# Gate operands of a two-layer decoder trunk: one of five formed in the gates, VectorE's gate steps in another order

## The reference

```python
    for i in range(DEPTH):                      # DEPTH = 2
        ...                                     # mixer of the layer, layer_norm
        hid = jnp.square(jax.nn.relu(jnp.einsum('bsd,df->bsf', x, ffn_w1[i])))
        x = layer_norm(DEEPNORM_ALPHA * x + jnp.einsum('bsf,fd->bsd', hid, ffn_w2[i]), ln2_g[i], ln2_b[i])
        gate = jax.nn.sigmoid(jnp.einsum('bsd,de->bse', x, ple_gate_w[i]))
        x = x + gate * jnp.einsum('bsk,kd->bsd', p[i], ple_w[i])
```

## Time and profile before

| | us |
|---|---|
| median of 3 runs | 2057.95 |
| lowest, highest | 2057.12, 2059.17 |
| profiled execution, own time | 2063.47 |
| profiled execution, span | 2061.7 |
| TensorE (PE) busy | 2036.8 |
| VectorE (DVE) busy | 1405.0 |
| ScalarE (ACT) busy | 890.9 |
| GpSimd (POOL) busy | 763.4 |

### The profile page before, as it was taken

How to read it: one execution, slowest core, us unless ns; L and a number is a source line. 1 busy time by engine, 2 the same in 40 slices (tenths; PEclk the granted TensorE clock), 3 DMA queues, 4 the chain that set the end, 5 groups by cost and what they waited for, 6 DMA issues and landing times.

```text
span 2061.7 us, 25116 instructions
## 1 busy us (share of the span) xinstructions
PE 2036.8 (99%) x9341; PEld 1689.1 (82%) x9341; DVE 1405.0 (68%) x1721; ACT 890.9 (43%) x1283; POOL 763.4 (37%) x505
## 2 busy tenths in 40 slices
PE   9999999999999999999999999999999999999999
PEld 9888788888888888787888888788888888887877
DVE  4744775655666868676887669775655666777595
ACT  3112465455544445352433343654444543445541
POOL 5212257777702000110367650268877412000200
PEclk9999999999999999999999999999999999999999
DMA  6121123444589896434122238033443599886343
GB/s 190 38 66 41 41 75 129 159 159 147 203 288 390 301 321 224 167 112 153 42 77 87 88 114 308 21 117 139 160 155 135 207 380 383 281 296 226 113 174 123
DMA packets 201366, 352.19 MB, mean 171 GB/s; under 512 B 14401, under 2 KB 72861, under 8 KB 198685
## 3 DMA queue, kind: packets, MB, share of 16 engines
q1 hardware_dynamic: 190432, 320.92, 44.5%
q10 hardware_dynamic: 10812, 29.67, 3.9%
HBM read 258.78 MB, written 91.75 MB: 170 GB/s over the span
## 4 chain that ended last, share of the span: by engine, by line
PE 79%; DVE 11%; issue 3%; POOL 3%; ACT 2%; DMA 1%; DVEq 0%; ACTq 0%; POOLq 0%
PE bank_a L2735 15%; PE bank_a L2737 15%; PE bank_a L2736 15%; PE bank_b L2735 10%; PE bank_b L2737 10%; PE bank_b L2736 10%; POOL op_lo L1457 2%; DVE hop_lo L2521 1%; DMA w_raw<-in_ffn_w_dram 1%; DVE wop_lo L2524 1%; PE bank_a L2774 1%; PE bank_b L2774 1%; POOL op_sum L1548 1%; DVE xt_lo L2021 1%; DVE xt_lo L2221 1%
## 5 line engine op out<-in xcount | busy, mean ns | idle before, releaser
L1444 POOL TENSOR_TENSOR w_lo<-raw,w_hi 128x512 fp32r<-128x512 f32 x84 | 118.3, 1440 | 694.6 <-ACT w_hi L1569 694.5
L1457 POOL TENSOR_TENSOR op_lo<-op_sum,op_hi 128x512 fp32r<-128x512 f32 x151 | 224.5, 1503 | 33.4 <-ACT op_hi L1891 27.5
L1891 ACT CAST op_hi<-op_sum 128x512 fp32r<-128x512 f32 x151 | 93.8, 621 | 328.9 <-POOL op_sum L1548 87.9
L1856 ACT CAST hop_hi<-h_raw 128x1024 fp32r<-128x1024 f32 x124 | 130.3, 1051 | 231.2 <-PE bank_a L2737 134.7
L2735 PE MATMUL bank_a<-wop_hi,hop_hi 128*128 128x512 f32 x576 | 224.4, 390 | 0.4 <-DVE resid L2543 0.4
L2736 PE MATMUL bank_a<-wop_lo,hop_hi 128*128 128x512 f32 x576 | 224.3, 389 | 0.0
L2737 PE MATMUL bank_a<-wop_hi,hop_lo 128*128 128x512 f32 x576 | 224.3, 389 | 0.0
L2521 DVE TENSOR_TENSOR hop_lo<-h_raw,hop_hi 128x1024 fp32r<-128x1024 f32 x124 | 152.0, 1226 | 97.4 <-ACT hop_hi L1856 97.2
L1457 POOL TENSOR_TENSOR op_lo<-w_raw,op_hi 128x512 fp32r<-128x512 f32 x115 | 164.1, 1428 | 116.9 <-ACT op_hi L1891 115.8
L2735 PE MATMUL bank_b<-wop_hi,hop_hi 128*128 128x512 f32 x432 | 171.0, 396 | 7.4 <-DVE resid L2546 7.4
L2737 PE MATMUL bank_a<-xt_hi,op_lo 128*128 128x512 f32 x456 | 177.6, 390 | 0.0
(11 more groups left out here) (275 smaller groups left out, 4940.7 us busy)
## 6 DMA issues: line engine op xcount, KB each, us to landing
w_raw<-in_ffn_w_dram SPq DMA_DIRECT2D x144, 512.0 KB, 6.7
h_raw<-h_spill SPq DMA_DIRECT2D x112, 512.0 KB, 6.5
h_spill<-h_tile SPq DMA_DIRECT2D x170, 256.0 KB, 2.1
w_raw<-in_ffn_w_dram SPq DMA_DIRECT2D x112, 256.0 KB, 3.5
gate_parts<-park_r ACTq DMA_DIRECT2D x40, 512.0 KB, 4.4
w_hi<-gate_parts SPq DMA_DIRECT2D x10, 1024.0 KB, 4.8
w_lo<-gate_parts SPq DMA_DIRECT2D x10, 1024.0 KB, 7.0
w_raw<-in_od_w_in_dram SPq DMA_DIRECT2D x40, 256.0 KB, 3.4
```

Of the source, the lines that this page charges most:

```text
L1444: pool.tensor_tensor(lo, raw[:, n % NRAW, :], hi.bitcast(F32), ALU.subtract).then_inc(lo_split, 1)
L1457: pool.tensor_tensor(by_four(op_lo[s]), operand_raw(tr, b, op), by_four(op_hi[s]).bitcast(F32), ALU.subtract).then_inc(op_low, 1)
L1856: act.copy(hop_hi[k][:, :, :], h_raw[a.hop_chunk(i)][:, :, :]).then_inc(ahead_hi, 1)
L1891: act.copy(by_four(op_hi[s]), operand_raw(tr, b, op)).then_inc(op_high, 1)
```

## The change

B22 is parked no more. Its raw quadrant is loaded at the start of the gates into a buffer of its own, ScalarE copies its high part behind form m6, and VectorE subtracts the low part in the program of form m5. The four sums left are formed in 10 steps per half, from items 24 and 34, with each store and copy at another step. In the gates VectorE leaves the affine of tiles 2 and 3 and the addition of their gated products out of m2's program and does them behind the lows of S1 and S4; the steps of m7 are reordered so that S4's sum comes before the split of X and S1's low before S4's. `gated` is cut in two for it, `times_bank` and `add_gated`.

```diff
--- before.py
+++ after.py
@@ -68,13 +68,14 @@
 GATE_X = ("S3a0", "S3a1", "S3b0", "S3b1", "S2r0", "S2r1", "S3l0", "S3l1", "S4a0", "S4a1", "S2l0", "S2l1",
-          "S1r0", "S1r1", "Xh0", "Xh1", "Xl0", "Xl1", "S4b0", "S4b1", "S4l0", "S4l1", "S1l0", "S1l1")
+          "S1r0", "S1r1", "S4b0", "S4b1", "Xh0", "Xh1", "Xl0", "Xl1", "S1l0", "S1l1", "S4l0", "S4l1",
+          "B22l0", "B22l1")
 GATE_W = ("P1l",)
-GATE_HIGH = ("S30", "S31", "S20", "S21", "S40", "S41", "S10", "S11", "P1")
-PARKED = ("B22", "T3", "T1", "T2", "T4")
-PARK_D = ("B22l", "T3r", "T1r", "T2r", "T3l", "T1l", "T4r", "T2l", "T4l")
-PARK_A = ("B22h", "T3h", "T1h", "T2h", "T4h")
-PARK_FROM, PARK_STEPS = 20, 13
+GATE_HIGH = ("S30", "S31", "S20", "S21", "S40", "S41", "S10", "S11", "B220", "B221", "P1")
+PARKED = ("T3", "T1", "T2", "T4")
+PARK_D = ("T3r", "T1r", "T2r", "T3l", "T1l", "T4r", "T2l", "T4l")
+PARK_A = ("T3h", "T1h", "T2h", "T4h")
+PARK_FROM, PARK_STEPS = 24, 10
...
@@ -773,6 +774,7 @@
         gate_dram = nc.dram_tensor("gate_parts", (2, len(PARKED), 2, P, 4, HALF), F32, kind="Internal").ap()
+        b22_raw = at("b22_raw", [P, 4, HALF], 160 * K1)
...
@@ -1280,6 +1282,10 @@
                 if name == "m1":
+                    last = heads[layer]["m4"]
+                    sp.wait_ge(b_full, last.gb + HT)
+                    rows = ple_gate_w[layer][HALF:2 * HALF, HALF:2 * HALF].rearrange("(q p) n -> p q n", p=P)
+                    sp.dma_start(b22_raw[:, :, :], rows).then_inc(gate_w_in[4], 16)
                     gate_product_done(sp, st, "m1")
                     part("T3", 0)
                 if name == "m2":
@@ -1290,9 +1296,6 @@
                     part("T1", 0)
                     rows = ple_w[layer][:, HALF:2 * HALF].rearrange("(q p) n -> p q n", p=P)
                     sp.dma_start(gp_raw[:, :, :], rows).then_inc(gate_w_in[5], 16)
-                if name == "m6":
-                    gate_product_done(sp, st, "m6")
-                    part("B22", 1)
                 if name == "m5":
                     gate_product_done(sp, st, "m5")
                     part("T4", 0)
@@ -1693,25 +1696,20 @@
                         park_stored(act, st, 0)
                     quarter(1, 1, park[0])
                     quarter(0, 1, park[1])
-                if s == 2:
-                    park_done(act, st, "B22l")
-                    store("B22", 2, 3)
+                    quarter(0, 0, park[2])
                 if s == 3:
-                    park_stored(act, st, 1)
-                    quarter(0, 0, park[2])
-                if s == 6:
                     park_done(act, st, "T3l")
                     store("T3", 3, 0)
-                if s == 8:
+                if s == 5:
                     park_done(act, st, "T1l")
                     store("T1", 3, 1)
-                if s == 9:
-                    park_stored(act, st, 3)
+                if s == 6:
+                    park_stored(act, st, 2)
                     quarter(1, 0, park[1])
-                if s == 11:
+                if s == 8:
                     park_done(act, st, "T2l")
                     store("T2", 0, 2)
-                if s == 12:
+                if s == 9:
                     park_done(act, st, "T4l")
                     store("T4", 3, 1)
@@ -1766,6 +1764,11 @@
                 if name == "m5":
+                    gate_product_done(act, st, "m6")
+                    act.wait_ge(gate_w_in[4], 16 * (layer + 1))
+                    hi, _ = gate_weights(layer, 1)
+                    for m in range(2):
+                        act.copy(pair_of(hi, m), pair_of(b22_raw, m)).then_inc(gate_high, 1)
                     gate_x_done(act, layer, "S1l1")
                     for k in range(HT):
                         copy_out("m5", k, g_sum[168][:, k, :])
@@ -1806,14 +1809,11 @@
                 if st.kind == "park":
                     load_and_park(st)
-                    form = {1: ("B22h", 2, 0), 4: ("T3h", 3, 0), 7: ("T1h", 3, 1), 8: ("T2h", 0, 2), 11: ("T4h", 3, 1)}.get(st.item)
-                    if form:
-                        name, dst, raw_w = form
-                        if name == "B22h":
-                            park_landed(act, st, 2)
-                        else:
-                            park_done(act, st, name[:2] + "r")
-                            park_stored(act, st, {"T3h": 1, "T1h": 2, "T2h": 2, "T4h": 3}[name])
+                    forms = {1: (("T3h", 3, 0),), 4: (("T1h", 3, 1), ("T2h", 0, 2)), 7: (("T4h", 3, 1),)}
+                    for name, dst, raw_w in forms.get(st.item, ()):
+                        park_done(act, st, name[:2] + "r")
+                        if name != "T3h":
+                            park_stored(act, st, {"T1h": 1, "T2h": 1, "T4h": 2}[name])
                         act.copy(park_r[dst][:, :, :], park[raw_w][:, :, :]).then_inc(park_high, 1)
...
@@ -2180,27 +2180,24 @@
                                       ALU.subtract).then_inc(park_step, 1)
 
                 if st.item == 1:
-                    low("B22h", 3, 0, 2)
-                if st.item == 2:
-                    park_done(dve, st, "B22l")
+                    park_landed(dve, st, 3)
                     step(park[0], park[0], park[1], ALU.subtract)
-                if st.item == 5:
-                    park_landed(dve, st, 3)
                     park_done(dve, st, "T3r")
                     step(park[1], park[1], park[2], ALU.subtract)
                     park_done(dve, st, "T1r")
                     step(park[2], park[0], park[2], ALU.add)
-                if st.item == 5:
+                if st.item == 2:
                     park_done(dve, st, "T2r")
                     low("T3h", 0, 0, 3)
+                if st.item == 4:
+                    low("T1h", 1, 1, 3)
                 if st.item == 7:
-                    low("T1h", 1, 1, 3)
-                if st.item == 10:
                     park_landed(dve, st, 4)
+                    park_done(dve, st, "T1l")
                     step(park[1], park[1], park[2], ALU.subtract)
                     park_done(dve, st, "T4r")
                     low("T2h", 2, 2, 0)
-                if st.item == 11:
+                if st.item == 8:
                     low("T4h", 1, 1, 3)
@@ -2236,13 +2233,19 @@
-                def gated(tile, ring, full, bank, t, n, read):
+                def times_bank(tile, ring, full, bank):
                     dve.wait_ge(b_full if ring == "B" else a_full, full)
                     dve.tensor_tensor(tile, tile, banks[ring][bank % RING][:, :], ALU.mult).then_inc(gate_read, 1)
+
+                def add_gated(tile, t, n, read):
                     r = resid[:, t, n * HALF:(n + 1) * HALF]
                     dve.wait_ge(gate_affine, 2 * TT * layer + 2 * t + 2)
                     dve.wait_ge(gate_read, gate_count(GATE_READS, layer, read))
                     dve.tensor_tensor(r, r, tile, ALU.add).then_inc(x_new, 1)
+
+                def gated(tile, ring, full, bank, t, n, read):
+                    times_bank(tile, ring, full, bank)
+                    add_gated(tile, t, n, read)
...
@@ -2275,30 +2278,34 @@
                     gate11(0, 3)
                     add11(3, 4)
                     gate11(1, 5)
-                    affine((2,))
-                    gate11(2, 6)
-                    affine((3,))
-                    gate11(3, 7)
+                    for k in (2, 3):
+                        sig_ready(f"s11{k}")
+                        times_bank(sig3[:, k % 3, :], "B", st.gb + 4 + k + 1, st.gb + 4 + k)
                 if name == "m7":
                     gate_product_done(dve, st, "m2")
                     x_step(g_part, xt12[0].bitcast(F32), g_sum[48], ALU.subtract, "S2r")
                     gate_x_done(dve, layer, "S4a1")
                     x_low(xt11[1], g_sum[48], xt11[0], "S2")
                     x_step(g_sum[168], g_sum[168], g_sum[176], ALU.add)
+                    x_step(g_sum[56], g_part, xt12[1].bitcast(F32), ALU.add, "S4a")
                     for m in range(2):
                         dve.tensor_copy(pair_of(xt22[0], m), pair_of(g_sum[176], m)).then_inc(gate_x, 1)
                     for m in range(2):
                         gate_x_done(dve, layer, f"Xh{m}")
                         dve.tensor_tensor(pair_of(xt22[1], m), pair_of(g_sum[176], m), pair_of(xt22[0], m).bitcast(F32),
                                           ALU.subtract).then_inc(gate_x, 1)
-                    x_step(g_sum[56], g_part, xt12[1].bitcast(F32), ALU.add, "S4a")
+                    gate_product_done(dve, st, "m7")
+                    x_low(s3[1], g_sum[168], s3[0], "S1")
                     x_low(xt12[1], g_sum[56], xt12[0], "S4")
                 if name == "m6":
-                    gate_product_done(dve, st, "m7")
-                    x_low(s3[1], g_sum[168], s3[0], "S1")
-                    affine(range(HT, HT + 2))
+                    for k in (2, 3):
+                        affine((k,))
```

(11 more changed lines are left out.)

## The result

The changed kernel takes 2078.37 us (median of 4 runs, 2077.23 to 2082.88), the kernel before 2058.16 in the same comparison. The ratio is 1.0102 with a 95% interval of 1.0085 to 1.0120, so the change costs about 21 us. The forecast was 2059.1, with a range of 2054 to 2067: the measured time lies outside it, on the slow side. The profiled execution has a span of 2081.1 us, 19.4 more than before.

The account below looks back on a forecast made before the run. TensorE was busy 2036.8 of 2061.7 us, so only its waits and lower-clock stretches could pay. Terms: -8.1 (feed-forward) - 1.8 (first-layer gates) + 11.0 (second-layer gates) = +1.1 on 2057.95, giving 2059.1 us; range 2054 to 2067.

Parts of the forecast that it names:

- the part on the feed-forward change: Parking without B22 in ten steps a half: first half free, second half's stores off critical loads, 8.1 us gained.
- the working for the seam: TensorE's wait at form m4 after m7, both layers: shrinks from 3.95 and 3.02 us to 1.5, bounds 0.5 and 4.8.
- rival 1: Feed-forward loads stay late at the m7 to m4 seam, no gain there: +9.2 us, 2067; chance 0.25.
- The estimate of 2 us: Feed-forward seam: stores of T2 and T4 delay item 49's w load by 2 us, making each wait 2.7, not 1.5.
- The gates of the first layer: Reordered VectorE steps remove TensorE's waits of 0.29 and 1.47 us ahead of forms m6 and m5: -1.8 us.
- The gates of the second layer: T1's load queues behind output stores on SyncE, TensorE stands 10 us before form m5: 8.3 plus 2.7 clock, +11.0 us.
- its 0.9 us: Second layer's gates: extra delay if the two 256 KB stores just ahead slow T1's load; not in the sum.
- the seam's gain: Feed-forward waits at form m4 after m7, clock included: 5.2 us in the first layer, 2.9 in the second, 8.1 in sum.
- the price of the queue: Second layer's gates, SyncE's stores ahead of T1's load: m5 begins 8.3 us later, plus 2.7 of clock, 11.0 us.
- The judgement "no change": Whole kernel: forecast +1.1 us; time within 0.2% (4.1 us) of the kernel before, chance 0.62.
- Rival 2: Second layer's gates: T1's load leaves when m7 is done despite the stores; -11.6 us, 2046.4; chance 0.07.
- Rival 3: Feed-forward seam at form m4 after m7: waits under 0.5 us; -1.9 us in sum, 2056; chance 0.13.

Follow-up runs that it names:

- e3: Changed kernel with eleven parking steps a half from item 22, T1's and T2's high copies two items behind T3's store: 2063.45 us, ratio 1.0015.
- e7: Changed kernel with eleven parking steps a half from item 22 and the output stores of tiles 2 and 3 behind T1's load: 2049.43 us, ratio 0.9942.
- e9: e7 with only the second half's stores of T2 and T4 issued two items later, where the kernel before had them: 2054.49 us, ratio 0.9973.
- e10: Changed kernel with its ten steps a half started from item 22, and stores of tiles 2 and 3 behind T1's load: 2052.31 us, ratio 0.9966.
- e1: Changed kernel with the second layer's output stores of tiles 2 and 3 behind the loads of T1 and gp_raw: 2065.53 us, ratio 1.0028.
- e8: Kernel before with only VectorE's new gate order and stores of tiles 2 and 3 behind T1's load, B22 still parked: 2056.23 us, ratio 0.9974.

## Why the prediction was wrong

**The step that failed** is this one, of the part on the feed-forward change: "The first half lies where TensorE never waits, and I cost it at nothing: preparations run four products (some 21 us) ahead, and that covers a ScalarE wait for a store, which is one product (5.4 us) long or less." Three things in it were wrong. The waits are not all 5.4 us long or less: the stores take 8.0 to 8.3, and where ScalarE comes late from one wait there are fewer than 5.4 us left to the next (6.73 and 6.22 were the longest). They are not one but four, 21.4 us in the first layer. And they reach from the end of the first half into the second half's first steps, which the working for the seam skipped: it took the end of ScalarE's squares, 797.7, from the trace of before and let that time stand, so that VectorE was to be done with item 45 at 801.0. It was done at 805.99. With ten steps VectorE entered 5.5 us later (8.7 in the second layer). The loss from it is 17.9 us (e3), and no rival had it: rival 1 expected late loads, by another mechanism.

Shift the prediction's working by the 5.5 us, and its additions begin at 839.3 instead of 833.8; they began at 839.14. That close agreement is in part luck. The load of w of item 49 left only 3.3 us later than in the working (818.06 for 814.8), so some of the delay had been taken up, and the loads then took longer than the working had them: 6.1 us for 5.3, and 5.1 for 4.1 for w of item 51.

**The seam's own working held in its result, not in each term.** The run from entry to additions came out 3.7 us shorter, and in e3 TensorE waits 0.42 and 1.33 us (0.41 and 1.25 in e7) for a forecast of 1.5 with bounds of 0.5 and 4.8, with the clock kept. e9 shows that the stores of T2 and T4 were the reason. In e3, though, VectorE enters 1.6 us earlier than before (45.6 us ahead of TensorE's readiness for 43.9, counted as in e10), which the working had not assumed, and its first load is slower than assumed. What the prediction drew from the Trainium skill (DMA: Bandwidth & Descriptors, "Issuing engines are not separate DMA queues") holds in sign here: in the changed kernel w of item 49, issued at 818.06 behind the stores, came after 6.1 us instead of 5.3. The estimate of 2 us was too high, 0.8 was measured here. In e3 the same load took 6.2 us (issued at 812.47, used at 818.70), but left 1.6 us ahead of the working's 814.8 when the zeros of the traces are matched, so the waits did not become 2.7.

**The gates of the first layer**: -1.8 forecast, and both waits are gone.

**The gates of the second layer**: +11.0 forecast, 9.95 of wait (11.71 - 1.76) and about 2.7 of clock measured in the profile. e1 gives 15.2 back, where the prediction's terms make 11.0 + 1.8 = 12.8. The place, the queue and the order were right. Of the 1.65 us by which the wait was short, 1.2 are the low half's landing time, 8.2 us instead of 7.0. The prediction had named the likely reason, the two stores just ahead, and left its 0.9 us out of the sum; no run tests it.

**The sum.** With a loss of 17.9 us that was not in it, 2059.1 becomes 2077, against 2078.37. This is close in part because smaller errors cancel: by e7, e8 and e1 the seam's gain was 6.6 us for 8.1 and the price of the queue 2.4 higher, but the gates without it gave 5.4 for 3.5. The judgement "no change" rested on a gain and a loss that would cancel. The gain was there to be had, but the same ten steps that bring it delay the entry more than they save. Rival 2 (SyncE's order does not bind) is refuted. Rival 3 (the seam wholly clean) is what e3 comes near to, not the changed kernel.

## What to carry to other kernels

When steps are packed closer, list for each wait how far ahead its DMA is issued, in steps and in us, and compare with the landing time in the trace. Do it for every wait of every half, also where the first engine in the chain seems idle: a lead of preparations is one reserve, and all delays draw on it. Start the working for a critical stretch from the time at which the engines enter it in the changed program, not from the time in the old trace. And when a result moves later, look for DMAs that wait for it in a queue that also carries loads: two of four stores moved behind one load were worth 15 us.
